# Routing of the expert layer from the residual: scaled router weights, diagonals, and a token table in two halves

## The reference, cut to what matters

```python
x = x + g1 * mix                                             # the output projection
h = _rmsnorm(x, p['norm_g'][l, 1]) * (1 + sc2) + sh2         # modulated hidden row
...
logits = (x @ w_router).astype(f32) + b_router.astype(f32)   # here x is h
top_v, top_i = lax.top_k(logits, TOP_K)                      # 2 of 8
gates = jax.nn.softmax(top_v, axis=-1)
...
for e in range(N_EXPERTS):
    y = y + comb[:, e:e + 1] * _swiglu(x, we1[e], we3[e], we2[e]).astype(f32)
```

## Time and profile before

| | us |
|---|---|
| median of 3 runs | 2254.54 (2252.7 to 2257.42) |
| the profiled execution, its own time | 2258.64 |
| its span, first to last instruction | 2256.9 |
| PE busy in the span | 2074.9 (92%) |
| PE weight loads | 1712.3 (76%) |
| DVE busy | 1309.1 (58%) |
| ACT busy | 997.4 (44%) |
| POOL busy | 179.3 (8%) |
| mean granted PE clock | 0.928 of full |

### The profile page before, as it was taken

How to read it: one execution, slowest core, us unless ns; L and a number is a source line. 1 busy time by engine, 2 the same in 40 slices (tenths; PEclk the granted TensorE clock), 3 DMA queues, 4 the chain that set the end, 5 groups by cost and what they waited for, 6 DMA issues and landing times.

```text
span 2256.9 us, 36646 instructions
## 1 busy us (share of the span) xinstructions
PE 2074.9 (92%) x14266; PEld 1712.3 (76%) x14292; DVE 1309.1 (58%) x2052; ACT 997.4 (44%) x1456; POOL 179.3 (8%) x271
## 2 busy tenths in 40 slices
PE   6999868798999999999998778978899999999996
PEld 4999635588999999998997445865566657788883
DVE  3667644254544544456576552555565667789985
ACT  5422126344424442435221253434454555678772
POOL 3000120110000000000000201111010010010102
PEclk8999669798999999999997697987999999999998
DMA  9222767633545454542222346216677788899995
GB/s 319 69 75 75 183 206 248 194 107 82 166 135 164 135 160 131 165 136 63 76 68 73 120 155 206 77 60 227 211 243 235 256 273 287 326 373 382 370 379 196
DMA packets 272094, 418.23 MB, mean 185 GB/s; under 512 B 21214, under 2 KB 216312, under 8 KB 271952
## 3 DMA queue, kind: packets, MB, share of 16 engines
q1 hardware_dynamic: 249984, 349.50, 46.7%
q0 software_dynamic: 21968, 66.72, 9.2%
HBM read 385.73 MB, written 29.59 MB: 184 GB/s over the span
## 4 chain that ended last, share of the span: by engine, by line
PE 81%; DMA 7%; DVE 5%; ACT 3%; issue 2%; SPq 1%; POOL 1%; ACTq 0%; PEldq 0%; DVEq 0%; PEld 0%; POOLq 0%
PE banks L932 77%; PE banks L936 4%; DMA weight_ring<-in_w_ada 2%; DVE scratch L2513 1%; DMA expert_ring<-in_we 1%; DVE region L2513 1%; DMA region<-region 1%; DMA mix_t<-region 1%; ACT scratch L1878 1%; ACT region_split L1878 1%; SPq L588 1%; ACT hidden_t L1878 1%; DMA scratch<-bias_rows 0%; DMA hidden_t<-h_rows,pass_tokens 0%; DVE weights_lower L2513 0%
## 5 line engine op out<-in xcount | busy, mean ns | idle before, releaser
L932 PE MATMUL banks<-upper_parts,region_split 128*128 128x320 f32 x1664 | 390.2, 310 | 4.5 <-DVE upper_parts L2513 4.5
L932 PE MATMUL banks<-upper_parts,weights_lower 128*128 128x320 f32 (+1 forms) x1248 | 386.8, 310 | 0.0
L2513 DVE TENSOR_TENSOR expert_lower<-expert_ring,region_split 128x1408 fp32r<-128x1408 f32 (+1 forms) x198 | 286.3, 1469 | 106.8 <-PE banks L932 78.7
L932 PE MATMUL banks<-region_split 128*128 128x320 f32 (+1 forms) x1264 | 341.8, 333 | 2.9 <-DVE upper_parts L2513 2.9
L932 PEld LDWEIGHTS banks<-upper_parts,region_split 128*128 128x128 f32 x1664 | 284.4, 188 | 4.8 <-issue 4.8
L1878 ACT ACTIVATE region_split<-expert_ring 128x1408 fp32r<-128x1408 f32 (+1 forms) x198 | 241.8, 1255 | 63.0 <-DMA expert_ring<-in_we 50.6
L932 PEld LDWEIGHTS banks<-region_split 128*128 128x128 f32 x1264 | 222.7, 188 | 25.0 <-issue 8.4
L932 PEld LDWEIGHTS banks<-upper_parts,weights_lower 128*128 128x128 f32 (+1 forms) x1248 | 235.1, 188 | 0.0
L932 PE MATMUL banks<-region_split,upper_parts 128*128 128x384 f32 x732 | 234.4, 384 | 0.1
L2513 DVE TENSOR_TENSOR weights_lower<-weight_ring,region_split 128x2048 fp32r<-128x2048 f32 (+2 forms) x72 | 168.9, 2350 | 96.2 <-ACT region_split L1878 96.1
L1878 ACT ACTIVATE region_split<-weight_ring 128x2048 fp32r<-128x2048 f32 (+2 forms) x72 | 140.6, 1958 | 164.2 <-PE banks L932 162.5
(11 more groups left out here) (333 smaller groups left out, 3285.6 us busy)
## 6 DMA issues: line engine op xcount, KB each, us to landing
expert_ring<-in_we SPq DMA_DIRECT2D x176, 704.0 KB, 6.4
expert_ring<-in_we SPq DMA_DIRECT2D x121, 512.0 KB, 4.7
weight_ring<-in_w_ada SPq DMA_DIRECT2D x48, 1024.0 KB, 9.9
weight_ring<-in_w SPq DMA_DIRECT2D x88, 512.0 KB, 4.9
weight_ring<-in_w_in SPq DMA_DIRECT2D x24, 1024.0 KB, 5.3
weight_ring<-in_w SPq DMA_DIRECT2D x16, 1408.0 KB, 6.3
weight_ring<-in_w_out SPq DMA_DIRECT2D x8, 1024.0 KB, 5.8
y_rows<-residual_t POOLq DMA_DIRECT2D x4, 1760.0 KB, 24.6
```

The lines of the kernel that those rows point to most:

```text
L932: return nc.tensor.matmul(out, lhsT, rhs, start=first, stop=last)
L2513: return v.tensor_tensor(out, x, y, op)
```

## The change

The logits and the token rows are made from the residual itself:

- The seven router loads are issued in out1, behind the pool loads and ahead of the K rows; the final gain row is loaded behind the first gather.
- DVE writes in out1 the samples' shifts spread over tokens (`SHIFT_SPREAD`) and eight diagonal matrices of the prompt's gains (`GAIN_DIAGONALS`), and later the router weights times the gain (`WRT_GAINED`). PE multiplies the shifts by the router weights (2 x 8 products of 8 columns) and DVE keeps them, with the router's bias, as `LOGIT_SHIFTS`.
- At the end of out1, behind the sums of squares, PE makes the logits with the tokens stationary: 5 tiles x 8 blocks, 128x8 each. DVE multiplies by the root and adds the shifts, two instructions. `spread_roots`, `scale`, `modulate` and the turning of the logits are gone in layer 1.
- The rows for DRAM are made by products of `XT` with the gain diagonals (for the samples a transpose of rows that DVE has already multiplied); ACT scales them by the root as it takes them out; POOL adds the shift row (`SHIFT_ROWS`, which PE and ACT make at the start of the stage), ten additions of 128x512.
- The one-hot matrices come ahead of the pass table and `slots_ready`; `OF_REST` is made in two pieces (128 and 32 slots), the two banks are handed over apart, and `TABLE` column 0 is copied and signalled apart, so that POOL can gather the 128 rows before the riders' column is there. The three gate instructions come last.

```diff
@@ POOL
+                if l % 2:
+                    load(router_in,
+                         (WRT[:, :, :], a["w_router"][l // 2, :, :].rearrange("(k p) e -> p k e", p=P)),
...
+                    pool.wait_ge(shift_rows_ready, 1)
                     for t in range(NT):
-                        pool.wait_ge(h_rows_ready, t + 1)
+                        for half in range(2):
+                            at = slice(half * TP, (half + 1) * TP)
+                            pool.wait_ge(rows_scaled, 2 * t + half + 1)
+                            nc.gpsimd.tensor_tensor(HRB[:, t, at], HRB[:, t, at], SHIFT_ROWS[:, t // NTP, at], ALU.add)\
+                                .then_inc(h_rows_ready, 1)
+                        pool.wait_ge(h_rows_ready, 2 * t + 2)
                         load(h_rows_out if t < NTP else moe_y_out, (d["h_rows"][tiles(t), :], HRB[:, t, :]))
...
+                    pool.wait_ge(table_ready, 1)
+                    pool.wait_ge(h_rows_out, 16 * NTP)
+                    pool.wait_ge(moe_y_out, 16)
+                    know(slice(0, 1), slice(0, 1), 1)
+                    gather()
+                    pool.wait_ge(table_ready, 2)
+                    know(slice(1, 2), slice(0, 1), 2)
+                    gather_riders()
+                    load(final_row_in, (FINAL_ROW, ...))
@@ PE, out stage
+                if l % 2:
+                    take(router_in, 112)
+                    take(router_gains_ready)
+                    for kind in range(2):
+                        for k in range(KD):
+                            columns = SHIFT_SPREAD[:, k, :] if kind else MOD[:, l, 3 * KD + k, 0:1].broadcast_to([P, P])
+                            ins = mm(PS[:, 6, 256 + kind * NE:256 + (kind + 1) * NE], columns, WRT[:, k, :], k == 0, k == KD - 1)
                 hand(ins, "dve", 6)
...
                 sums_of_squares(f"out{l}")
+                if l % 2:
+                    wait(residual_ready, RESIDUALS_BEFORE[f"out{l}"] + KD)
+                    wait(router_gains_ready, 2)
+                    claim(1)
+                    for t in range(NT):
+                        if t == NTP:
+                            take(sample_gained)
+                        for k in range(KD):
+                            ins = mm(PS[:, 1, t * NE:(t + 1) * NE], XT[:, k, tiles(t)] if t < NTP else XGS[:, k, :],
+                                     WRT_GAINED[:, k, :] if t < NTP else WRT[:, k, :], k == 0, k == KD - 1)
+                    hand(ins, "dve", 1)
                 stage(f"out{l}")
-                spread_roots()
+                if l % 2 == 0:
+                    spread_roots()
@@ PE, route stage
-                    take(router_in, 128)
...
-                    turn_hidden(0)
-                    take(logits_out)
...
+                    for u, b in enumerate((2, 3, 6, 7)):
+                        kind, half = divmod(u, 2)
+                        claim(b)
+                        for j in range(4):
+                            k = 4 * half + j
+                            columns = SHIFT_SPREAD[:, k, :] if kind else MOD[:, l, 3 * KD + k, 0:1].broadcast_to([P, P])
+                            ins = mm(PS[:, b, tiles(j)], columns, ident[:, :], True, True)
+                        hand(ins, "act", b)
+                    def turn_gained(t):
+                        for half in range(2):
...
+                                if t < NTP:
+                                    ins = mm(PS[:, b, tiles(j)], XT[:, k, tiles(t)], GAIN_DIAGONALS[:, k, :], True, True)
+                                else:
+                                    ins = tr(PS[:, b, tiles(j)], XGS[:, k, :])
+                    turn_gained(0)
+                    turn_gained(1)
                     take(masks_ready)
...
@@ ACT, route stage
+                            drained(func(HRB[:, t, half * TP:(half + 1) * TP], PS[:, 4 + (2 * t + half) % 4, :], ACT.Identity,
+                                         scale=ROOT[:, t:t + 1]))
+                            also(rows_scaled)
@@ DVE, out stage
-                    v.memset(WRT[:, :, :], 0.0)
+                    copy(SHIFT_SPREAD.rearrange("p k (b t) -> p k b t", t=TS), by_token(3)).then_inc(router_gains_ready, 1)
+                    tt(GAIN_DIAGONALS, along(ident[:, :], 1, KD), along(MOD[:, l, 4 * KD:5 * KD, 0], 2, P), ALU.mult)
                 lower(0)
@@ DVE, route stage
+                    drained(tt(RLG[:, :, 0:NE], PS[:, 1, 0:NT * NE]..., along(ROOT, 2, NE), ALU.mult), True)
+                    link(tt(RLG[:, :, 0:NE], RLG[:, :, 0:NE], LOGIT_SHIFTS[:, :, :], ALU.add))
```

More of the change, by code:

```diff
@@ L852, in store_riders @@
                                            YB_RIDERS[32 * g:32 * (g + 1), :]).then_inc(rider_y_out, 16)
[L854 to L859, removed]
+                    pool.wait_ge(table_ready, 1)
[6 more added lines that the diff above has]
+                    gather_riders()
+                    load(final_row_in, (FINAL_ROW, a["final_g"].rearrange("(one n) -> one n", one=1).broadcast_to([P, D])))
+                    ridden = pool.value_load(PASSES[0:1, RIDDEN_TRIPS_AT:RIDDEN_TRIPS_AT + 1],
+                                             min_val=LEAST_RIDDEN - 2, max_val=MOST_RIDDEN - 2)
+                    trips = pool.value_load(PASSES[0:1, TRIPS_AT:TRIPS_AT + 1], min_val=LEAST_PASSES - 2, max_val=MOST_PASSES - 2)
+                    for first in (1, 2):
+                        pool.wait_ge(tokens_known, first + 1)
+                        pool.wait_ge(rows_turned, 2 * first)
+                        pool.wait_ge(riders_turned, first)
+                        know(slice(0, 2), slice(first, first + 1), first + 2)
+                        gather()
                         gather_riders()
                     def steady(i, ridden_gather):
-                        pool.wait_ge(tokens_known, i + 3)
+                        pool.wait_ge(tokens_known, i + 4)
                         pool.wait_ge(rows_turned, i * 2 + 6)
@@ L1537, in _ @@
                     hand(mm(PS[:, 3, 64:64 + NE], ones[:, :], MSUM[:, NT, :], True, True), "dve", 3)
-                    turn_hidden(3)
-                    turn_hidden(4)
+                    for t in range(2, NT):
+                        turn_gained(t)
                     for u, (t, half) in enumerate(EARLY_ROWS):
@@ L2262, in _ @@
                 if l % 2:
-                    for k in range(KD):
-                        modulate(k, mod(l, 4, k)[:, 0:1], mod(l, 3, k)[:, 0:1])
-                if l % 2:
-                    take(for_act)
-                    copy(LOGT[:, 0:TP], PS[:, 0, :])
-                    drained(copy(LOGT[:, TP:], PS[:, 1, 0:P]))
-                    also(logits_out)
+                    for u, b in enumerate((2, 3, 6, 7)):
+                        kind, half = divmod(u, 2)
+                        take(for_act)
+                        drained(copy(SHIFT_ROWS[:, kind, half * TP:(half + 1) * TP], PS[:, b, :]))
+                    also(shift_rows_ready)
                     for t in range(NT):
@@ L3043, in _ @@
                 if l % 2:
-                    tt(by_sample(XGS), by_sample(XT[:, :, SAMPLE]), sample_vectors(l, 4), ALU.mult)
-                inverse_roots()
+                    tt(by_sample(XGS), by_sample(XT[:, :, SAMPLE]), sample_vectors(l, 4), ALU.mult).then_inc(sample_gained, 1)
+                    for x in (RLG, RT8, RU8):
+                        v.memset(x[:, :, :], MARK)
+                    take(root_ready)
+                    link(v.reciprocal(ROOT, ROOT))
+                else:
+                    inverse_roots()
                 stage(f"out{l}")
@@ L3166, in _ @@
                     link(tt(GB[:, :], GA[:, :], E2[:, :], ALU.mult))
-                    take(for_dve)
-                    copy(TABLE[:, 0, :], PS[:, 0, 0:MAX_PASSES])
-                    drained(copy(TABLE[0:RIDERS, 1, :], PS[0:RIDERS, 1, 0:MAX_PASSES]))
-                    also(table_ready)
                     stage(f"route{l}")
```

118 lines of the change are left out of this document (50 added, 68 removed).

## The result

The changed kernel takes **2269.87 us** (median; 2264.52 to 2277.69), the kernel before 2254.54, each over five executions (the table above says three): ratio **1.0071**, 95% interval 1.0049 to 1.0094. It is slower, as forecast, but by 15.3 us where the forecast said 9.0, and 0.4 us outside its range.

A forecast was written before the change was run, and what follows sets the result against it. PE was taken as busy 92% of the span, the change touching only a dependent chain at 1420 to 1550 us; 4.7 - 1.1 + 4.1 - 3.1 - 0.6 + 5.0 = +9.0 on 2254.5 gave 2263.5 us, range 2248.5 to 2269.5.

The forecast's parts named there:

- Output stage, +4.7: Layer 1's output stage: 3.6 us for PE's 32 narrow instructions, 0.9 for a clock dip, 0.2 on DVE; +4.7 us.
- P to MAX, -1.1: From 1488.87, leaving the dense products, to MAX: 80 logit instructions, mostly at 1.2 GHz, make 20.6 us against 21.7.
- Rivals 2 and 3: Logits and shift rows: clock stays 2.4 GHz; DVE held, 2252.7 us (chance 0.09), or free, 2247.7 us (chance 0.12).
- M to C, +4.1: From MAX's start to the token-count copies: PE first makes shift rows and two token tiles, so DVE waits; +4.1 us.
- C to the one-hots without the hold, -3.1: From the token-count copies to the first one-hot products: pass table moved behind, fewer columns compared ahead; 9.3 us, -3.1.
- GpSimd, +5.0: Beside DVE's chain from the count copies on: 5 to 6 GpSimd additions at 0.9 us hold DVE; +5.0 us.
- Rival 4: GpSimd's shift-row additions are slow, 1.4 us each: 9.8 us in place of 5.0, total 2268.3 us; chance 0.10.
- One-hots to turned rows, -0.6: From one-hot products to first turned rows: gather issued 1.2 us earlier, PE's late rows limit the gain; 16.9 us, -0.6.
- The delay of SP's expert loads costed at nothing: Expert loads begin some 5 us behind the one-hots instead of 2 ahead; used only after the stage, so no cost.
- Turned rows to the dense products: Last stretch, from the turned rows to the first dense product: no term, 9.9 us before and forecast.

The follow-up runs named there:

- e1: The changed kernel with GpSimd's ten additions of the shift row left out; ratio 1.0024 to the kernel before.
- e7: The changed kernel with each half of a prompt row tile stored by its own DMA, so GpSimd never makes two additions back to back; ratio 1.0087 to the kernel before.
- e3: The changed kernel with the pass table, the slots and their signal to SyncE ahead of the one-hot matrices again; ratio 1.0060 to the kernel before.
- e10: The changed kernel run once more, nothing altered, beside the same runs of the kernel before; ratio 1.0078.
- e4: The changed kernel with the logits as wide products, router weights stationary and tokens moving; ratio 1.0033 to the kernel before.

## Why the prediction was wrong, step by step

- **Output stage, +4.7: right** (+5.1, and +3.5 in the other execution). The 32 narrow instructions took 3.57 us for 3.6. The dip of the clock behind them, put at 0.9 between bounds of 0 and 1.7, was 1.5 us in one execution (granted clock 0.62 from 1426 to 1430) and none in the other (1.00), so that the middle came near is luck.
- **P to MAX, -1.1: right** (-0.5, and -2.4 in the other execution). The clock was 0.50 through the logits, as the stretch of 19-column products had it. Rivals 2 and 3 fell here: PE was busy for 17 of 17 us and granted 0.50. One reading was wrong without harm to the sum: of the 57 us from P the prediction says 1.2 GHz over nearly all, where the mean granted clock is 0.67.
- **M to C, +4.1: right** (+4.8 and +3.4).
- **C to the one-hots without the hold, -3.1: right** (-3.0 in e1). The lengths given there, 12.5 and 9.3, make -3.2.
- **GpSimd, +5.0: this step failed in its size.** e1 gives 11.0 us. The addition took 1.25 us where I took 0.9 (the estimate from the figure in the Trainium skill, GPSIMD Engine Reference, Elementwise, was 1.1). More than that, I had "5 to 6 of them" slip into gaps: VectorE's chain has no gap as long as an addition, so each of the four pairs behind C is paid whole. Four pairs at 2.5 are 10, and the four long rows of the chain, 2.87 + 2.93 + 2.94 + 2.82 less 0.2 each, are 10.8. The upper bound, 8.4, was also too low, for it had seven additions at 1.2. The mechanism itself, which no row of before showed in this direction, came out as the Trainium skill (SBUF — State Buffer, Who interferes with whom) has it, the lock held for the whole instruction (1.5 us beside single additions of 1.27 in e7); that two instructions in a row can hold it together is what I had not reckoned with. Rival 4 had the size nearly right (+9.8) for a neighbouring reason.
- **One-hots to turned rows, -0.6: this step failed in its sign** (+2.1). "The delay of SP's expert loads costed at nothing" looked at PE's and ScalarE's order of work, and not at how fast the places fill: loads issued together land one by one, ScalarE waits for each of the first four (after the first, 0.47, 1.26 and 2.03 us, the last at 1550.70), its evictions stand behind them in its queue, and PE waits for those. Before, SP began them at 1526.85, 9.5 us ahead of ScalarE's first one at 1536.38; now it is 4.0 (1538.78 and 1542.81). With the old order, in e3, the length fell from 19.6 to 16.2. The gather was not what failed: it was issued 5.9 us behind the start of the one-hots, 2.8 earlier than before, where I had reckoned with 1.2.
- **Turned rows to the dense products**, taken as unchanged, +1.2 in one execution and -3.1 in the other: the granted clock was 0.58 from 1556 to 1565 in the one and 1.00 over this stretch in the other.

The local terms add up to +20.8 in one execution of the changed kernel and +11.3 in the other, +16 between them, and the medians say +15.3. The forecast's own mistakes are 6.0 and 2.7, 8.7 together, of which the time shows 6.3.

## What to carry to other kernels

Before giving GpSimd an elementwise job on two SBUF inputs, ask whether VectorE then stands in a chain of small dependent instructions: here it paid the whole duration of every GpSimd instruction beside that chain, and splitting the stores didn't help. MAX8 and MATCH_REPLACE8 ran on beside them. Count narrow products by instructions (0.22 us each here at 1.2 GHz with 128 stationary columns), not by columns: put the few columns on the stationary side and the many on the moving side even if that costs an eviction and a second sum. When a signal is moved behind other work, follow what it starts to its landing and look at the queue in which its consumer stands.

## What the runs showed of the hardware that was not expected

An untouched stretch can differ by more than the change. Up to layer 1's output stage both kernels are the same program. Yet this stage begins at 1422.75 us in the kernel before, at 1410.80 in the changed kernel and at 1428.64 in e10, the changed kernel again. Most of the first difference arises in layer 1's mixer, where the changed kernel was 2.6 us ahead at 1376 and 12 at 1411. Ten us from there, before and after (the same stage, not the same instructions):

```profile
1380.00:1390.00 10.00, 9.56 (x89) 6.07 (x89) 1.68 (x5) 3.37 (x10) 1.95 (x3) 0.50 0.44 137
```

```profile
1380.00:1390.00 10.00, 8.84 (x158) 6.10 (x152) 3.08 (x10) 4.40 (x16) 3.48 (x6) 1.00 0.70 212
```

PE was granted 1.2 GHz in the one and 2.4 GHz in the other; the same 48 instructions of 16 columns took 2.75 us there before (1383.66) and 1.58 after (1380.21). The 35 executions of the kernel before beside e1 to e4 ran from 2245.7 to 2272.6 us. A change of 10 us is settled here by medians over many executions, and its parts only by lengths between landmarks.
